# Modulation vectors computed with the conditioning as the stationary operand, in four column groups, and the late ones in the second half of the first expert sweep

## The reference, cut to what matters

```python
mod_l = (jax.nn.silu(c) @ ada_w[l] + ada_b[l])[:, None, :]        # ada_w[l]: 1024 x 6144
mod_c = jax.nn.silu(c_ctx) @ ada_w[l] + ada_b[l]
sh1, sc1, g1, sh2, sc2, g2 = jnp.split(mod_l, N_MOD, axis=-1)
...
a_lat = modulate(rmsnorm(h_lat, norm1_g[l]), sh1, sc1)
...                                                                # mixer, h = h + g1 * y
def block(args):                                                   # over blocks of tokens
    act = jax.nn.gelu(jnp.einsum('tkd,td->tk', U[it], xt), approximate=False) * gt
    return jnp.einsum('tk,tkd->td', act, V[it])
```

## Time and profile before

| | us |
|---|---|
| median of three runs | 3646.95 (3642.12 to 3654.03) |
| the profiled execution, its own time | 3648.24 |
| its span in the profile | 3646.4 |
| TensorE busy | 3426.9 (94%) |
| VectorE busy | 1979.2 (54%) |
| ScalarE busy | 1191.8 (33%) |

### The profile page before, as it was taken

How to read it: one execution, slowest core, us unless ns; L and a number is a source line. 1 busy time by engine, 2 the same in 40 slices (tenths; PEclk the granted TensorE clock), 3 DMA queues, 4 the chain that set the end, 5 groups by cost and what they waited for, 6 DMA issues and landing times.

```text
span 3646.4 us, 47438 instructions
## 1 busy us (share of the span) xinstructions
PE 3426.9 (94%) x19384; PEld 2917.3 (80%) x19384; DVE 1979.2 (54%) x3330; ACT 1191.8 (33%) x1795; POOL 20.0 (1%) x41
## 2 busy tenths in 40 slices
PE   8899897999999999999999999798468999999998
PEld 7465546888888888888888888688458999999998
DVE  2204633488855555634444444333935998856665
ACT  1111224322233333333333333424314444444443
POOL 0000000000000000000000000000000000000000
PEclk9889898999999999999999999899789999999999
DMA  5241012355555556576556655222014777788885
GB/s 175 70 128 46 1 41 95 114 168 162 166 166 199 193 182 203 173 246 201 192 190 193 193 190 161 69 83 91 0 58 157 211 212 243 246 275 265 266 260 168
DMA packets 232862, 587.87 MB, mean 161 GB/s; under 512 B 21239, under 2 KB 104264, under 8 KB 229000
## 3 DMA queue, kind: packets, MB, share of 16 engines
q1 hardware_dynamic: 227536, 528.57, 46.2%
q0 software_dynamic: 4208, 53.27, 3.8%
q10 hardware_dynamic: 904, 3.01, 0.2%
HBM read 483.06 MB, written 101.71 MB: 160 GB/s over the span
## 4 chain that ended last, share of the span: by engine, by line
PE 87%; DVE 10%; ACT 2%; issue 1%; DMA 1%; ACTq 0%; SPq 0%; DVEq 0%
PE ps L501 42%; PE ps L743 30%; PE ps L657 7%; PE ps L699 5%; DVE w_lo L1459 1%; PE ps L556 1%; DVE arena L1376 1%; PE ps L618 1%; PE ps L679 1%; DVE arena L1370 1%; PE ps L807 0%; PE ps L626 0%; ACT a_t L890 0%; DVE arena L1611 0%; DVE arena L1378 0%
## 5 line engine op out<-in xcount | busy, mean ns | idle before, releaser
L1459 DVE TENSOR_TENSOR w_lo<-wring,w_hi 128x1024 fp32r<-128x1024 f32 x512 | 626.0, 1223 | 736.5 <-ACT w_hi L1008 735.0
L501 PE MATMUL ps<-a_hi,w_hi 128*128 128x512 f32 (+1 forms) x2048 | 703.6, 344 | 8.5 <-DVE w_lo L1459 4.4
L743 PE MATMUL ps<-act_hi,w_hi 128*128 128x512 f32 (+1 forms) x2048 | 697.6, 341 | 3.4 <-DVE act_lo L1490 3.4
L501 PE MATMUL ps<-a_hi,w_lo 128*128 128x512 f32 (+1 forms) x2048 | 690.5, 337 | 0.0
L501 PE MATMUL ps<-a_lo_q,w_hi 128*128 128x512 f32 (+1 forms) x2048 | 690.0, 337 | 0.0
L743 PE MATMUL ps<-act_lo,w_hi 128*128 128x512 f32 (+1 forms) x2048 | 688.8, 336 | 0.0
L743 PE MATMUL ps<-act_hi,w_lo 128*128 128x512 f32 (+1 forms) x2048 | 688.3, 336 | 0.0
L1008 ACT CAST w_hi<-wring 128x1024 fp32r<-128x1024 f32 x512 | 534.3, 1044 | 226.3 <-PE ps L743 226.2
L501 PEld LDWEIGHTS ps<-a_hi,w_hi 128*128 128x128 f32 x2048 | 390.0, 190 | 48.6 <-DVE w_lo L1459 7.0
L743 PEld LDWEIGHTS ps<-act_hi,w_hi 128*128 128x128 f32 x2048 | 388.5, 190 | 50.1 <-issue 3.6
L501 PEld LDWEIGHTS ps<-a_hi,w_lo 128*128 128x128 f32 x2048 | 389.6, 190 | 42.0
(11 more groups left out here) (226 smaller groups left out, 3597.4 us busy)
## 6 DMA issues: line engine op xcount, KB each, us to landing
wring<-in_u SPq DMA_DIRECT2D x256, 512.0 KB, 4.1
wring<-in_v SPq DMA_DIRECT2D x256, 512.0 KB, 4.1
gates<-arena POOLq DMA_DIRECT2D x24, 2048.0 KB, 7.6
acts<-arena SPq DMA_DIRECT2D x128, 256.0 KB, 4.6
arena<-acts SPq DMA_DIRECT2D x128, 256.0 KB, 3.5
arena<-gates SPq DMA_DIRECT2D x16, 2048.0 KB, 11.4
aring<-in_ada SPq DMA_DIRECT2D x56, 512.0 KB, 5.1
wring<-in_ada SPq DMA_DIRECT2D x40, 512.0 KB, 3.7
```

What stands on the lines that cost most here:

```text
L501: ins = pe.matmul(o, l, r, start=n == 0, stop=n == len(pairs) - 1, **kw)
L743: ins = pe.matmul(value_sum(l, c), w, x, start=m == 0 and n == 0 and (l == 0 or c % 2 == 0), stop=m == NKEY - 1 and n == 2, skip_group_che ...
L1459: tt(WLO[:, k % 4].rearrange("p k n -> p (k n)"), wring[:, n % RING * TILE:(n % RING + 1) * TILE], WHI[:, k % 4].rearrange("p k n -> p (k ...
```

## The change

The two conditioning rows become the stationary operand. They lie in `cpad`, which has 32 columns for each of the eight slices, all zero but the first two. `rows(g, ...)` takes two tiles at once: eight products with a stationary operand of 128x32 and 256 moving weight columns; slice k writes to PSUM partitions 32 (k mod 4) onward, so the products go to four column groups of the array in turn, and slices k and k + 4 add up in one place. ScalarE copies the 128 x 256 result to `arows` (`rows_in`). `turned(g)` then makes columns of it: two products with 128 columns of `arows` as stationary operand and `rowsel` moving, a 128 x 2 table with ones at rows 0, 32, 64, 96 and 1, 33, 65, 97, which sums the four column groups and turns the rows. VectorE adds the bias from there, two tiles at a time.

There are 8 pairs at the start, 12 in `ab_in` and 28 late ones. A pair must lie in neighbouring slots of the ring, so in `ab_in` it goes ahead of the projection tile where it would wrap (`ada_leads`, at j = 2, 6 and 10). The late pairs move to turns 56, 58, ... 110; their ring is now in the arena, where two token tiles of the routing lay, so SP waits for the routing's end before the first. The PSUM bank of a pair waits for the copy two pairs back (late ones share one bank and wait for the last copy).

```diff
@@ constants
-ADA_GROUPS = ([(4 * g, 4, AT_ADA + 4 * g) for g in range(ADA_FIRST // 4)]
-              + [(ADA_FIRST + ADA_AB * j, ADA_AB, at_abin(j) + 1) for j in range(AB_GROUPS)])
-FIRST_GROUPS = ADA_FIRST // 4
+def ada_leads(j):
+
+    return j < AB_GROUPS and (AT_ABIN + 3 * j + 1) % RING == RING - 1
+FIRST_GROUPS = ADA_FIRST // 2
-LATE_TURN = {2 * j + 1: j for j in range(ADA_LATE)}
-LATE_TAKEN = {2 * LATE_GROUP * (g + 1): g for g in range(LATE_GROUPS)}
+LATE_TURN = {FIRST_OCT + 2 + 2 * j: j for j in range(LATE_GROUPS)}
@@ SP
             def late(j):
 
-                wait(sp, S["late_used"], j - 1)
-                sp.dma_start(aring[:, j % 2 * TILE:(j % 2 + 1) * TILE], a["ada"][LATE_AT + j])\
-                    .then_inc(S[f"late_loaded{j % 2}"], 16)
+                m = 2 * (EARLY_GROUPS + j)
+                sp.wait_ge(S["gates_ready"], TT)
+                wait(sp, S["late_used"], 2 * (j - 1))
+                sp.dma_start(LATE_W[j % 2].rearrange("p r k n -> p r (k n)"),
+                             a["ada"][m:m + 2].rearrange("r p n -> p r n")).then_inc(S[f"late_loaded{j % 2}"], 16)
@@ TensorE, filters()
                 group(ps[0:64, 0, 0:256], [(FW1, ZPOS)], "f_proj")
-                ada(2)
+                ada(4)
+                turned(3)
+                ada(5)
+                turned(4)
                 pe.wait_ge(S["f_sin"], 1)
                 group(ps[0:64, 1, 0:256], [(FW2, FHID[0])], "f_proj")
-                ada(3)
+                ada(6)
+                turned(5)
+                ada(7)
+                turned(6)
+                turned(7)
                 pe.wait_ge(S["f_sin"], 2)
-                pe.wait_ge(S["ada_taken"], 4)
+                pe.wait_ge(S["ada_taken"], FIRST_GROUPS)
@@ TensorE
+            def rows(g, w, done):
+
+                bank = 5 + g % 2 if g < EARLY_GROUPS else 5
+                wait(pe, S["rows_in"], g - 1 if g < EARLY_GROUPS else g)
+                for k in range(KD):
+                    q = 32 * (k % 4)
+                    ins = pe.matmul(ps[q:q + 32, bank, 0:256], CP[:, k, :], w[:, :, k, :], start=k < 4, stop=k >= 4)
+                ins.then_inc(S[done], 2)
+            def turned(g):
+
+                if g == 0:
+                    pe.wait_ge(S["sel_ready"], 1)
+                pe.wait_ge(S["rows_in"], g + 1)
+                wait(pe, S["ada_taken"], g)
+                for x in range(2):
+                    ins = pe.matmul(ps[:, 4, 2 * x:2 * x + 2], arows[:, 256 * (g % 2) + P * x:256 * (g % 2) + P * x + P],
+                                    rowsel[:, :], start=True, stop=True)
+                ins.then_inc(S["rows_turned"], 1)
@@ TensorE, ab_in()
+                    if ada_leads(j):
+                        ada(FIRST_GROUPS + j)
...
-                    if j < AB_GROUPS:
+                    if j < AB_GROUPS and not ada_leads(j):
                         ada(FIRST_GROUPS + j)
+                    if 1 <= j <= AB_GROUPS:
+                        turned(FIRST_GROUPS + j - 1)
@@ TensorE, first_products()
                     if l == 0 and m in LATE_TURN:
+                        if m - 2 not in LATE_TURN:
+                            pe.wait_ge(S["slots_in"], TT)
                         late(LATE_TURN[m])
+                    if l == 0 and m - 1 in LATE_TURN:
+                        turned(EARLY_GROUPS + LATE_TURN[m - 1])
@@ ScalarE
+            def rows_in(g):
+
+                if g < EARLY_GROUPS:
+                    act.wait_ge(S["w_used"], ADA_AT[g] + 2)
+                else:
+                    act.wait_ge(S["late_used"], 2 * (g - EARLY_GROUPS + 1))
+                wait(act, S["rows_turned"], g - 1)
+                bank = 5 + g % 2 if g < EARLY_GROUPS else 5
+                copy(arows[:, 256 * (g % 2):256 * (g % 2) + 256], ps[:, bank, 0:256]).then_inc(S["rows_in"], 1)
...
+            for g in range(4):
+                rows_in(g)
             filters()
@@ VectorE
             def ada(g):
-                m, count, pos = ADA_GROUPS[g]
-                dve.wait_ge(S["w_used"], pos + count)
-                tt(M2[:, m:m + count, :], ps[:, 5 + g % 2, 0:2 * count].rearrange("p (m z) -> p m z", z=2),
+                dve.wait_ge(S["rows_turned"], g + 1)
+                tt(M2[:, 2 * g:2 * g + 2, :], ps[:, 4, 0:4].rearrange("p (m z) -> p m z", z=2),
@@ VectorE, first_products()
-                    if l == 0 and m in LATE_TAKEN:
-                        late(LATE_TAKEN[m])
+                    if l == 0 and m - 3 in LATE_TURN:
+                        ada(EARLY_GROUPS + LATE_TURN[m - 3])
```

More of the change, by code:

```diff
@@ L181, in build @@
         small = sb("small", 16)
-        aring = sb("aring", 2 * TILE)
+        cpad = sb("cpad", KD * 32)
+        rowsel = sb("rowsel", 2)
+        arows = sb("arows", 2 * 256)
         ps = ctx.enter_context(nc.psum_tensor("ps", [P, 8, 512], F32))
@@ L267, in build @@
         RB = [view(2048, "p (b g e t) -> p b g e t", b=2, g=groups(l), e=BLK, t=GTOK) for l in range(2)]
+        LATE_W = [over(f"late_ring{b}", at, 2 * TILE, F32)[:, :].rearrange("p (r k n) -> p r k n", r=2, k=KD)
+                  for b, at in enumerate(PS_AT[2:])]
         ZIN = view(12288, "p (r t) -> p r t", r=ZRING, t=T)
@@ L387, in stream, with stream_abin, ab @@
                     load(n0 + j, row(src, r0 + j))
[L389 to L396, removed]
-            def late(j):
-                wait(sp, S["late_used"], j - 1)
-                sp.dma_start(aring[:, j % 2 * TILE:(j % 2 + 1) * TILE], a["ada"][LATE_AT + j])\
-                    .then_inc(S[f"late_loaded{j % 2}"], 16)
+            def stream_abin():
+                def ab(j):
+                    load(at_abin(j), a["abin"][j])
+                for j in range(N_ABIN):
+                    if not ada_leads(j):
+                        ab(j)
+                    if j < AB_GROUPS:
+                        for x in range(2):
+                            load(at_ada_ab(j) + x, a["ada"][ADA_FIRST + ADA_AB * j + x])
+                    if ada_leads(j):
+                        ab(j)
+            def late(j):
+                m = 2 * (EARLY_GROUPS + j)
[3 more added lines that the diff above has]
+                             a["ada"][m:m + 2].rearrange("r p n -> p r n")).then_inc(S[f"late_loaded{j % 2}"], 16)
             def z_load(l, m):
@@ L828, in _ @@
             ada(0)
-            ada(1)
+            for g in range(3):
+                ada(g + 1)
+                turned(g)
             filters()
@@ L872, in filters @@
                     act.activation(FHID[n], FARG, ACT.Sin).then_inc(S["f_sin"], 1)
+                    for g in range(4 + 2 * n, 6 + 2 * n):
+                        rows_in(g)
                 for t in range(2):
@@ L916, in ab_in @@
                     copy(dst, ps[:, j % 4, :]).then_inc(S["ab_taken"], 1)
+                    if j < AB_GROUPS and not ada_leads(j):
+                        rows_in(FIRST_GROUPS + j)
                     c = j - 1
@@ L1185, in filters @@
                     ts(FARG, FARG, 3.1415925, -3.1415925, ALU.min, ALU.max).then_inc(S["f_arg"], 1)
-                ada(2)
-                ada(3)
+                    for g in range(3 + 2 * n, 5 + 2 * n):
+                        ada(g)
+                ada(7)
                 for n in range(8):
@@ L1647, in readout @@
                         .then_inc(S["mx_ready"], 1)
-            dve.wait_ge(S["consts_in"], 16 * len(first))
+            row_selector()
             bounds()
             key_numbers()
-            ada(0)
-            ada(1)
+            for g in range(3):
+                ada(g)
             filters()
-            gains_of([0], 4)
+            gains_of([0], FIRST_GROUPS)
             norm(0, T)
```

55 lines of the change are left out of this document (28 added, 27 removed).

## The result

| | before | after |
|---|---|---|
| median, us | 3647.54 (four runs) | 3706.31 (four runs, 3703.55 to 3708.23) |
| span of the profiled execution | 3646.4 | 3701.8 |
| TensorE busy | 3426.9 (94%) | 3371.4 (91%) |

A forecast was written before the change was run, and what follows sets the result against it. TensorE, busy 94% of the span, was taken as the bound. Start -12, projection -25, late work -30 + 4, wait +94.5, clock +20 gave +52 on 3648.2: 3700, median 3699 us; range 3645 to 3775, held at 0.8.

The forecast's parts named there:

- likeliest case: The forecast's own case for the whole kernel: 3699 us, stated range 3665 to 3735, chance 0.55.
- start: Modulation products at the kernel's start, pairs at half clock: 12 us gained, bounds 22 gained and 10 lost.
- projection: Input projection's first twelve tiles and groups: 145 us become 120, a gain of 25 if the clock holds.
- late work: Sweep: 56 late tiles (102.5 us) become 28 pairs (73 us), 30 us off, with 4 given back.
- wait: Sweep: TensorE's turning products wait for VectorE's addition of the previous late pair, 27 times 3.5 us, 94.5 us added.
- the last of the prediction's own signs: For the pairs' records: the prediction is wrong if the overlap is far from two at a time.
- clock behind the wait: Sweep: records at half clock after the idle time, 0 to 27 x 1.8 = 49 us, taken as 20.
- the wait isn't there: Rival for the sweep: VectorE adds the previous pair before TensorE asks; 3584 us, chance 0.05.
- The overlap: Within each pair on TensorE: 16 records take 9 steps, 1.95 us, or 2.15 us with entering and leaving the 32-column form.
- four groups at once: Rival for every pair: products of four column groups run concurrently, 1.07 us, a pair 1.5; 3651 us, chance 0.12.
- The price of a lead: Projection, three places where a pair leads: second tile lands 4.0 us later behind 2.6 us of work, 4 us in all.
- VectorE in the first half: First half of the sweep: VectorE's limited slack, after 27 late tiles leave, gives back 4 us, bounds 0 and 20.

The follow-up runs named there:

- Experiment 1: Changed kernel with VectorE's addition of a late pair moved ahead of the turn's one-hot tables: 3549.8 us, 0.9733 of before.
- experiment 2: Changed kernel with VectorE's addition of a late pair placed between the turn's two one-hot tables: 3614.2 us in one run.
- experiment 3: Changed kernel with 15 unused products of 128x512 put ahead of TensorE's wait in each waiting turn: 3646.25 us, 0.9995 of before.
- experiment 5: Kernel of Experiment 1 with all eight products of a pair in one column group: 3639.4 us in one run.
- experiment 6: Kernel of Experiment 1 with a pair's products going in turn to two column groups: 3567.7 us in one run.
- experiment 4: Kernel of Experiment 1 with each two consecutive products of a pair going to the same column group, four groups as before: 3552.6 us in one run.

## Why the prediction came out right, and where its steps did not

Forecast 3699, measured 3706.3, inside the likeliest case's own range. The sign and the largest term are right for the reason given. The closeness is luck for the larger part: start, projection, late work and wait together came out 43 us cheaper than forecast, and the clock 48 us dearer. By the last of the prediction's own signs, that it is wrong if the overlap is far from two at a time, its account of the pair was wrong: four records ran at a time.

| term | forecast | measured |
|---|---|---|
| start | -12 | -20.8 |
| projection | -25 | -26.9 |
| late work | -30, +4 | -54.6 |
| wait | +94.5 | +90.3 |
| clock behind the wait | +20 | +68 |

- **The wait: right in place, count and size.** 27 times, between L584 and L1286, 3.35 us each, from exactly the rows used: the two tables stand between the one-hot products and the addition. Experiment 1 takes it away by moving one addition of 0.15 us ahead of two tables, and the gain that the forecast's rival "the wait isn't there" described is there: 3549.8, even below its 3584, since the pairs are cheaper than assumed.
- **The clock behind it: right mechanism, mis-sized term, above its upper bound of 49.** I had taken 1.8 us of loss from the earlier trace rows and thought it would strike in fewer than half of the turns. It struck in all 27, and in 13 of them it was 3.3 us. The one wait of the earlier trace rows, 1.95 us long, was no bound for one of 3.35 us; experiment 2 shows that a shorter one of 1.48 us does lose 1.6 us in about half of the turns. That small products of the same turn without idle time lose nothing (1.83 us in the sweep before) was right, by experiments 1 and 3.
- **The overlap: the step that failed.** "Only the second of one product and the first of the next can overlap" gave 9 steps and 2.15 us; 1.00 us was measured, and 1.23 us with what it adds around it. What happened is the rival "four groups at once" (1.07 us), given 0.12. The Trainium skill (TensorE: Matmul & The Clock Gate, Part 3) said that small products at different column groups run concurrently; by experiments 5 and 6 the trace agrees, with 1.93 times for two groups and 3.57 for four. The argument against it, that the two records of a product share a group, doesn't hold, whatever the order (experiment 4). The rival's own sum, 3651, is off by the clock: with 48 us more there, 8 for the leads of the projection, 1.5 at the start and in the late work, and 4 less of wait, it is 3704; the profiled execution's own time is 3703.55. Of the 0.2 us for entering and leaving the 32-column form, no run shows that it is the change of form: beyond four steps of 0.216 us a pair takes 0.14 us, and the record behind a pair starts as late (0.34 us instead of 0.23) as one behind two-column products (0.33), where the form doesn't change.
- **The start.** With pairs of 1.9 us at half clock instead of 4.2 the ring sets the pace, as the prediction had said for full clock. Gain 20.8, beside the bound of 22.
- **The projection.** Right by cancelling: a step was 8.5 us instead of 9.5, so 12 less, but the leads cost 16 instead of 4. The price of a lead had only the landing in it, not the half clock that its idle time leaves behind (8.35 to 9.11 us for a tile) nor the wait of the tile behind.
- **VectorE in the first half** gave nothing back, where I had 4: 27 late tiles left turns 1 to 55, 27 x 1.83 = 49.4 us, and 49.7 are gone. Its slack sufficed.
- **The range** of the likeliest case was narrower than its terms: 0 to 49 for the clock and 10 to either side for start and projection give 3659 to 3748, not 3665 to 3735. The measured time lies in both.
- The gain of the change's parts, 102 us in the ledger and 98 in experiment 1, was real. It went into a wait that an addition's place on VectorE made, and into the clock.

## What to carry to other kernels

When a product is made to wait for a short operation of another engine, read what stands ahead of that operation on its engine, and what that waits for: here two tables of 3.1 us stood between, and they hung on the waiting engine's own last work, so the wait was certain. Put the short operation ahead of them. And price idle time on TensorE with what follows it: here 3.35 us of idle, between 1.8 us of one-hot products and the two-column ones, cost another 2.5 us of half clock each time.

## What the runs showed of the hardware that I had not expected

- Four column groups of 32 columns make float32 products 3.57 times as fast (16 records of 256 columns in 1.00 us instead of 3.57), and it makes no difference (1.00 or 1.02) whether consecutive products go to different groups or two by two to the same one. The Trainium skill (TensorE: Matmul & The Clock Gate, Part 3) also says that products start and end in strict program order; by that, and with records of one group behind each other, 2.8 us were due. The measurement decides. The trace doesn't name the group of a record, but records start four at a time, by inference one of each group, and so not in program order; what brings this about stays open.
- Idle time of 1.48 us, behind 1.8 us of one-hot products, was enough to bring the granted clock down in 13 of 27 turns. Putting 3.4 us of useless work into the 3.35 us wait made the kernel 60 us faster.
- With longer work at the start the clock was higher: with one group instead of four a pair takes 3.6 times as long at equal clock, but the start became only 6.6 us longer (44.2 to 50.8 us). Most of it ran at 2.4 GHz instead of 1.2, and 6.6 us less were idle.
